# Norm, skip and gating of the recurrent heads: from a stage of their own into the loop over the heads

## What is computed

```python
xc = silu(conv(xm) + conv_b)
h_f = mlstm_chunkwise(q, k, v, g[0], g[1])
h_b = flip(mlstm_chunkwise(flip(q), flip(k), flip(v), flip(g[2]), flip(g[3])))
hs = h_f + h_b                                  # per head, 1024 x 192
mu, var = mean(hs, -1), mean((hs - mu) ** 2, -1)
hs = (hs - mu) * rsqrt(var + LN_EPS)
hs = hs.transpose(...).reshape(B, S, 768) * norm_g
y = (hs + skip * xc) * silu(z)
return concatenate([y, memory_attention(q_mem, mem_k, mem_v)], -1)
```

## Time and profile before

| | us |
|---|---|
| median of three runs (lowest, highest) | 3457.37 (3456.45, 3463.05) |
| the profiled execution, its time | 3455.56 |
| the profiled execution, its span | 3453.8 |
| PE busy in it | 3174.3 (92%) |
| DVE busy | 1901.2 (55%) |
| ACT busy | 1361.8 (39%) |
| POOL busy | 393.6 (11%) |
| granted TensorE clock, mean over the span | 0.959 |

### The profile page before, as it was taken

The page is one execution under the profiler, slowest core; times in us unless marked ns, Lnnn a source line. Parts: engine busy times, 40 slices in busy tenths (PEclk is TensorE's granted clock), DMA queues, the critical chain, the costliest instruction groups (busy, mean ns, idle before and its releaser), DMA issues. The chain is left out here.

```text
span 3453.8 us, 50897 instructions
## 1 busy us (share of the span) xinstructions
PE 3174.3 (92%) x19659; PEld 2529.7 (73%) x19659; DVE 1901.2 (55%) x3571; ACT 1361.8 (39%) x2508; POOL 393.6 (11%) x313
## 2 busy tenths in 40 slices
PE   7999988999989988948799999699989989998999
PEld 6895566888867766747588888488855678895557
DVE  4536746757747725574656647634356543435564
ACT  2006841656652134334156546601344430134451
POOL 0100020333330000002023323200000000000000
PEclk9999998999999999979899999899999999999999
DMA  6518223868866300012368858610000220100012
GB/s 216 186 43 237 67 110 122 353 266 334 341 264 183 111 21 1 1 37 110 132 236 330 330 209 310 239 32 26 25 17 1 100 92 31 38 25 17 1 57 103
DMA packets 192934, 462.48 MB, mean 134 GB/s; under 512 B 44147, under 2 KB 119239, under 8 KB 184137
## 3 DMA queue, kind: packets, MB, share of 16 engines
q1 hardware_dynamic: 174281, 392.35, 31.6%
q0 software_dynamic: 18432, 67.12, 5.1%
HBM read 383.38 MB, written 73.33 MB: 132 GB/s over the span
## 5 line engine op out<-in xcount | busy, mean ns | idle before, releaser
L1790 PE MATMUL psum<-high_in,e_rowsT_high 128*128 128x256 f32 (+1 forms) x1080 | 329.8, 323 | 5.4 <-DVE e_rowsT_low L172 5.4
L1791 PE MATMUL psum<-high_in,e_rowsT_low 128*128 128x256 f32 (+1 forms) x1080 | 326.1, 320 | 0.0
L172 POOL TENSOR_TENSOR low_down<-w_down,high_out 128x1024 fp32r<-128x1024 f32 x64 | 206.7, 3248 | 298.3 <-ACT high_out L1868 298.3
L1790 PEld LDWEIGHTS psum<-high_in,e_rowsT_high 128*128 128x128 f32 x1080 | 206.4, 191 | 22.4 <-issue 6.2
L1791 PEld LDWEIGHTS psum<-high_in,e_rowsT_low 128*128 128x128 f32 x1080 | 206.6, 191 | 16.1
L3607 DVE CUSTOM_DVE_ANT_0 mla_probs<-psum,mla_mask 128x512 f32<-128x512 f32 (+2 forms) x192 | 96.9, 554 | 108.7 <-PE psum L3472 108.1
L172 DVE TENSOR_TENSOR low_gate<-w_gate,high_in 128x1024 fp32r<-128x1024 f32 x128 | 148.0, 1218 | 7.5 <-ACT high_in L1868 6.6
L172 DVE TENSOR_TENSOR low_up<-w_up,high_in 128x1024 fp32r<-128x1024 f32 x128 | 147.9, 1216 | 0.0
L1795 PE MATMUL psum<-low_up,e_rowsT_high 128*128 128x256 f32 x720 | 130.4, 283 | 0.0
L1868 ACT ACTIVATE high_out<-w_down 128x1024 fp32r<-128x1024 f32 x128 | 124.7, 1049 | 7.3 <-DMA w_down<-in_exp_w_down 7.3
L1868 ACT ACTIVATE high_in<-w_gate 128x1024 fp32r<-128x1024 f32 x128 | 124.8, 1058 | 6.2 <-issue 6.2
(11 more groups left out here) (592 smaller groups left out, 7592.0 us busy)
## 6 DMA issues: line engine op xcount, KB each, us to landing
w_gate<-in_exp_w_gate SPq DMA_DIRECT2D x32, 2048.0 KB, 8.4
w_up<-in_exp_w_up SPq DMA_DIRECT2D x32, 2048.0 KB, 13.5
w_down<-in_exp_w_down SPq DMA_DIRECT2D x32, 2048.0 KB, 20.3
ada<-in_ada_w SPq DMA_DIRECT2D x24, 1024.0 KB, 7.6
expert_rows<-e_out POOLq DMA_DIRECT2D x47, 512.0 KB, 7.0
expert_rows<-zero_row SPq DMA_DIRECT2D x33, 512.0 KB, 6.9
token_rows<-x SPq DMA_DIRECT2D x32, 512.0 KB, 2.6
x<-token_rows SPq DMA_DIRECT2D x24, 512.0 KB, 6.9
```

Source lines behind the costliest of these rows:

```text
L172: return eng.tensor_tensor(low, whole, high, ALU.subtract)
L1790: pe.matmul(dst, rows_high[:, k, :], w_high[:, k, cols], start=(k == 0), stop=False)
L1791: pe.matmul(dst, rows_low[:, k, :], w_high[:, k, cols], start=False, stop=False)
```

## The change

The norm's stage is gone; its work is put into the stage of the heads, and the preparation of the next head is put into another order.

- **Preparation.** The spreads go with the qk items of u = 0, 2, 4, 6, the raw items to u = 9 and 10, the keys to u = 8 and 11 to 13. DVE's masks come at u = 1, 3, 5, 7, ACT's exponentials two at a time at u = 4 to 11, `weigh` at u = 12 and 14. Head 0 is prepared in the same order.
- **DVE, every head.** From u = 8 on, the statistics of the unit before and the aggregate of the unit before that. At u = 4 of heads 1 to 3 it inverts the root of the head before, and at u = 6, 8, 9, 10 it normalises two pieces of that head each. After the loop come the last head's norm, and adding and gating for feature tiles 4 and 5.
- **ACT.** A root at u = 2 of heads 1 to 3. In the last head Silu of z at u = 3 to 8, the turned halves of tiles 0 to 3 times the gain into an SBUF tile (`hn_scaled`), and skip times xc for tiles 4 and 5.
- **PE.** In the last head the transposes of tiles 0 to 3, four at a time at eight units; those of tiles 4 and 5 after the loop.
- **GpSimd, new.** For tiles 0 to 3: xc times skip, plus `hn_scaled`, times the gate, each on 128x1024; then the gate of tile 4.
- **SP.** z is loaded in two parts (2 MB when the last keys product of the last head is done, 1 MB after that).

Cut to its core (the removed `head_norm` stands above):

```diff
@@ HeadItems
-        self.steps = [[("qk", u)] for u in range(8)] + [[("keys", m), ("spread", m)] for m in range(4)] + [[("raw", 0)], [("raw", 1)], [], []]
+        self.steps = [[qk[0], spread[0]], [qk[1]], [qk[2], spread[1]], [qk[3]], [qk[4], spread[2]], [qk[5]], [qk[6], spread[3]], [qk[7]],
+                      [keys[0]], [raw[0]], [raw[1]], [keys[1]], [keys[2]], [keys[3]], [], []]
+        self.order = [item for step in self.steps for item in step]
+        self.mask_at = {1: 0, 3: 1, 5: 2, 7: 3}
+        self.weigh_at = {12: 0, 14: 1}
+        self.exponents_at = {4 + n: (2 * n, 2 * n + 1) for n in range(DIRS * TILES // 2)}
@@ heads
+    EARLY_TILES = 4
+    TURN_AT = {4: 0, 5: 1, 7: 2, 8: 3, 10: 4, 11: 5, 12: 6, 13: 7}
+    NORM_AT = {6: (0, 1), 8: (2, 3), 9: (4, 5), 10: (6, 7)}
+    SILU_AT = {3 + f: f for f in range(ML_TILES)}
+    SKIP_AT = {9: 4, 10: 5}
+    late_units = [(4, 0), (5, 0), (4, 1), (5, 1)]
@@ sync
+            sp.wait_ge(s["keys_ready"], 4 * ML_HEADS)
+            sp.dma_start(zT[:, 0:EARLY_TILES, :], core.gate_rows[:, 0:EARLY_TILES, :]).then_inc(s["z_loaded"], 16)
+            sp.wait_ge(s["z_loaded"], 16)
+            sp.wait_ge(s["intra_ready"], U * LAST)
+            sp.dma_start(zT[:, EARLY_TILES:, :], core.gate_rows[:, EARLY_TILES:, :]).then_inc(s["z_loaded"], 16)
@@ tensor
+            def turn(dst, f, half):
+                pe.wait_ge(s["normed"], TILES * last_head_of(f) + 4 * half + 4)
+                for k in range(4):
+                    mm = pe.transpose(dst[:, k * P:(k + 1) * P], features(4 * half + k, f), c["ident"])
+                mm.then_inc(s["turned"], 1)
...
+                    elif u in TURN_AT:
+                        k = TURN_AT[u]
+                        pe.wait_ge(s["keys_copied"], 4 * ML_HEADS)
+                        if k >= 2:
+                            pe.wait_ge(s["scaled"], k - 1)
+                        turn(bank[4 + k % 2], *divmod(k, 2))
@@ scalar
+            def root(h):
+                act.wait_ge(s["variances_ready"], TILES * (h + 1))
+                act.activation(rstd[:, h, :], mv[:, h, :, 1], ACT.Sqrt, bias=c["eps_ln"]).then_inc(s["deviations_ready"], 1)
...
+                    if f >= 2:
+                        act.wait_ge(s["summed"], f - 1)
+                    act.activation(scaled[:, f % 2, half * BANK:(half + 1) * BANK], bank[4 + k % 2], ACT.Copy, scale=gain[:, f:f + 1]).then_inc(s["scaled"], 1)
@@ vector
+                    g = U * h + u
+                    statistics(g - 1)
+                    variance(g - 2)
+                    if h and u == 4:
+                        invert(h - 1)
+                    if h and u in NORM_AT:
+                        normalise(h - 1, NORM_AT[u])
+                    if h < LAST:
+                        prepare(h + 1, u)
...
+            invert(LAST)
+            normalise(LAST, range(TILES))
+            dve.wait_ge(s["skipped"], 2)
+            for n, (f, half) in enumerate(late_units):
+                q = slice(half * BANK, (half + 1) * BANK)
+                dve.wait_ge(s["turned"], 2 * EARLY_TILES + n + 1)
+                dve.scalar_tensor_tensor(out=xcT[:, f, q], in0=bank[4 + n], scalar=gain[:, f:f + 1], in1=xcT[:, f, q], op0=ALU.mult, op1=ALU.add).then_inc(s["added"], 1)
             dve.wait_ge(s["silu_done"], ML_TILES)
...
+            dve.wait_ge(s["added"], 4)
+            dve.tensor_tensor(xcT[:, 5, :], xcT[:, 5, :], zT[:, 5, :], ALU.mult).then_inc(s["gated"], 1)
@@ gpsimd
+            for f in range(EARLY_TILES):
+                x = xcT[:, f, :]
+                pool.tensor_tensor(x, x, skip[:, f:f + 1].to_broadcast([P, SEQ]), ALU.mult).then_inc(s["pool_steps"], 1)
+                pool.wait_ge(s["pool_steps"], f + 1)
+                pool.wait_ge(s["scaled"], 2 * f + 2)
+                pool.tensor_tensor(x, x, scaled[:, f % 2, :], ALU.add).then_inc(s["summed"], 1)
+                pool.wait_ge(s["summed"], f + 1)
+                pool.wait_ge(s["silu_done"], f + 1)
+                pool.tensor_tensor(x, x, zT[:, f, :], ALU.mult).then_inc(s["gated"], 1)
+            pool.wait_ge(s["silu_done"], EARLY_TILES + 1)
+            pool.wait_ge(s["added"], 3)
+            pool.tensor_tensor(xcT[:, 4, :], xcT[:, 4, :], zT[:, 4, :], ALU.mult).then_inc(s["gated"], 1)
```

More of the change, by code:

```diff
@@ L2060, in ml_layer @@
     heads(nc, core, xcT, wq, vals, table, hs)
-    head_norm(nc, core, hs, xcT)
     memT = m.at("ml_memT", W + 40 * KB, [P, 2, SEQ])
@@ L2325, in __init__ @@
     def __init__(self):
[L2326 to L2329, removed]
         self.per_head = {"qk": 8, "keys": 4, "spread": 4, "raw": 2}
-        self.steps = [[("qk", u)] for u in range(8)] + [[("keys", m), ("spread", m)] for m in range(4)] + [[("raw", 0)], [("raw", 1)], [], []]
+        qk, keys, spread, raw = [[(kind, i) for i in range(n)] for kind, n in self.per_head.items()]
+        self.steps = [[qk[0], spread[0]], [qk[1]], [qk[2], spread[1]], [qk[3]], [qk[4], spread[2]], [qk[5]], [qk[6], spread[3]], [qk[7]],
[4 more added lines that the diff above has]
+        self.exponents_at = {4 + n: (2 * n, 2 * n + 1) for n in range(DIRS * TILES // 2)}
     def count(self, kind, H, i):
@@ L2367, in heads @@
     den = m.at("r_den", W + 62 * KB, [P, U])
+    stats = m.at("hn_stats", W + 30 * KB, [P, ML_HEADS, TILES, 6])
+    mv = m.at("hn_mv", W + 30 * KB + 768, [P, ML_HEADS, TILES, 2])
+    rstd = m.at("hn_rstd", W + 31 * KB, [P, ML_HEADS, TILES])
+    gain = m.at("hn_gain", W + 31 * KB + 128, [P, ML_TILES])
+    skip = m.at("hn_skip", W + 31 * KB + 192, [P, ML_TILES])
+    spare = m.at("hn_spare", W + 31 * KB + 256, [P, 1])
+    zT = m.at("hn_z", W, [P, ML_TILES, SEQ])
+    scaled = m.at("hn_scaled", W + 40 * KB, [P, 2, SEQ])
+    LAST = ML_HEADS - 1
+    EARLY_TILES = 4
[4 more added lines that the diff above has]
+    late_units = [(4, 0), (5, 0), (4, 1), (5, 1)]
     bank, c, E = core.bank, core.c, table.E
@@ L2469, in copy_item, with exponents @@
                     act.activation(raw[:, 4 * i:4 * i + 4, :].rearrange("p c q -> p (c q)"), src, ACT.Copy).then_inc(s["raw_copied"], 1)
-            def exponents(H, d):
-                for chunk in range(TILES):
+            def exponents(H, u):
+                for n in items.exponents_at[u]:
+                    d, chunk = divmod(n, TILES)
                     if chunk % 4 == 0:
@@ L2499, in _ @@
                                        scale=E[:, IEXP * S + j:IEXP * S + j + 1]).then_inc(s["carried_ready"], 1)
[L2500 to L2504, removed]
+                    if u == DIRS and h:
+                        root(h - 1)
+                    if u >= 0:
+                        if h < LAST:
+                            prepare(h + 1, u)
+                        else:
+                            finish(u)
+            root(LAST)
         @block.vector
```

159 lines of the change are left out of this document (77 added, 82 removed).

## The result

| | before | after |
|---|---|---|
| median of five runs (lowest, highest) | 3459.68 (3456.45, 3463.05) | 3423.41 (3422.18, 3425.01) |
| the profiled execution, its span | 3453.8 | 3420.5 |
| PE busy | 3174.3 | 3172.5 (93%) |
| DVE busy | 1901.2 | 1906.2 (56%) |
| ACT busy | 1361.8 | 1370.3 (40%) |

The ratio is 0.9896, with a 95% interval from 0.9882 to 0.9909: 36 us faster. The forecast of 3417.3 us was 6 us too low: the time lies in the range from 3398 to 3432, but 1.4 us above the forecast's own range of 3408 to 3422, and next to the 3424 of the first rival.

A forecast was written before the change was run, and what follows sets the result against it. PE bounds heads with a successor, DVE the last head; PE also waits 16.8 us for `weigh`. Gains 23.9 + 32.8, less 16.6 for the port, give 40.1 us: 3417.3 us, own range 3408 to 3422, wider range 3398 to 3432.

The forecast's parts named there:

- first rival: Last head: POOL also holds normalisations and the output below u = 8; 7 us more, 3424; chance 0.18.
- Preparation and boundaries: Stage start to head 3: preparation 28.7, three heads 153.9, boundaries 1.5 us; head 3 starts at 184.1, gaining 23.9.
- Last head without POOL: Last head's 16 units, DVE the bound: 28.3 us, 5.9 added, 4.1 left over from before; together 38.3 us.
- The rest, 8.6 with the barrier: Behind the last head's loop: norm, four additions and a gate, 7.8 us, and the barrier, 0.8.
- The port: Last head and end: POOL operations hold DVE operations with two SBUF tensors; 15 us, plus 1.6 at the end.
- the sign that the prediction set itself: Last head: normalisations and output below u = 8 also showing 2 us and more would mean the first rival holds.
- At the end, gate against gate: After the last head: DVE's gate of tile 5 is held by POOL's gate of tile 4, 1.6 us.
- POOL's median: Last head: POOL's operations were to show a median above 2.36 us.
- the forecast's 247.6 us: The stage: 287.7 us before, less the forecast gain of 40.1 us.
- slower rival: Last head: POOL's chain sets the end from 7.2 us per operation; at 8 us the time is 3467; chance 0.03.
- the boundary wait: Rival, between heads: the order doesn't remove PE's wait for `weigh`; 19 us come back, 3436; chance 0.05.

The follow-up runs named there:

- order_alone: Kernel before with only the new preparation order, the norm keeping its own stage: 3433.75 us, ratio 0.9944.
- pool_tiny: Changed kernel with each of POOL's 13 operations cut to 2 of 1024 columns, leaving work out: 3381.87 us, ratio 0.9785, not usable as a time.
- pool_halves: Changed kernel with each POOL operation done as two of 512 columns, nothing left out: 3415.66 us, ratio 0.9893.
- dve_adds: Changed kernel without POOL: ScalarE skips all six tiles, DVE adds the turned halves from their banks and gates: 3414.52 us, ratio 0.9886.
- skip_on_act: Changed kernel with the skips of tiles 0 to 3 moved from POOL to ScalarE, units 0 to 3 of the last head: 3417.88 us, ratio 0.9894.
- after_again: The changed kernel itself, unaltered, timed once more beside its variants on one chip: 3421.29 us, ratio 0.9900.
- fold: Changed kernel without POOL, the skip folded into the turn by diagonal matmuls on TensorE, DVE finishing each half in one operation: 3415.18 us, ratio 0.9890.
- skip_early: Changed kernel with the skips of tiles 0 to 3 on ScalarE, all in units 0 and 1 of the last head: 3413.41 us, ratio 0.9881.
- fold_early: As fold, with the four diagonal matmuls of the late halves issued ahead of all turns: 3412.04 us, ratio 0.9873.
- norm_alone: Changed kernel with the old preparation order, the norm, skip and gate staying inside the heads' loop: 3445.76 us, ratio 0.9964.

## Why the prediction came out as it did

**Preparation and boundaries** were right. Head 3 was to start at 184.1 us; it does at 184.06 to 184.13 us in order_alone, pool_tiny, pool_halves, dve_adds and skip_on_act. That it fits to 0.1 us is luck, though: two small errors cancel. In order_alone PE is busy for 182.6 us of the 184.1 where my sum has 181.8 (heads take 51.7 us of PE's time for my 51.3), and idle for 1.5 where it has 2.35 (boundaries take 0.3 for my 0.5). In the changed kernel itself it is 188.25, for two reasons outside the sum: 3.3 us of slow clock and 0.9 us of a hold in head 2.

The slow clock first. PE's timeline at the start of the stage, in the changed kernel and then in pool_halves:

```profile
1269.29 2.45 PE L2436 MATMUL psum<-ml_xcT,ml_wqkv 128*96 128x512 f32 x4 [2.94 <-PEq L84]
1271.67 2.07 PE L2447 MATMUL psum<-neg_uT,consts 64*128 64x128 f32 x8
1273.68 5.50 PE L2436 MATMUL psum<-ml_xcT,ml_wqkv 128*96 128x512 f32 x8
```

```profile
1266.17 1.93 PE L2436 MATMUL psum<-ml_xcT,ml_wqkv 128*96 128x512 f32 x4 [2.94 <-PEq L84]
1268.03 1.15 PE L2447 MATMUL psum<-neg_uT,consts 64*128 64x128 f32 x8
1269.11 3.67 PE L2436 MATMUL psum<-ml_xcT,ml_wqkv 128*96 128x512 f32 x8
```

The same instructions behind the same idle time of 2.94 us take 9.8 and 6.55 us; the granted clock is 0.50 (1.2 GHz) for about 6 us in the first and 1.00 in the second. Of the ten traces with the new order four show the drop whole (after, after_again, fold, skip_early), fold_early in half, and five not at all. So the new order alone doesn't bring it, and norm_alone, with the old order, has half of it too (clock 0.94, PE busy 29.54 us for 27.85 before). In the changed kernel it came in both traces, which two traces can't tell from chance. Every trace that reaches the stage later than 1268.6 us has it, and of the others only fold_early (1266.21); whether that means anything no run tests. What decides is open.

**Last head without POOL**: 38.3 was forecast and 39.78 measured in pool_tiny. The missing part is ScalarE: DVE waits 2.4 us for carried copies there, a wait that I put at nothing beside 20 us of busy time in a head. The rest, 8.6 with the barrier, took 9.51: the four additions came 0.81 us apart and not 0.7. That is half of the difference; the rest is spread over the other parts.

**The port**: 15 forecast, 15.6 measured in the last head. That POOL holds DVE was right; which operations it holds was wrong, and the sum was right by luck, with two errors of about one size. I had priced only DVE operations with two SBUF tensors; they lost 9.1 us. The other 6.5 us fell on those with one tensor, the first rival's kinds. By the sign that the prediction set itself, maxima of 2 us and more in the normalisations and in the output below u = 8, it is the first rival that holds. It was right on what is held and wrong on the price: it took the loss for each POOL operation to rise towards 2.0 us, and it was 1.4 (15.6 / 11). In these rows a POOL operation holds DVE at most once, from the start of the first operation of the kinds above, and what DVE does freely between two holds (0.5 us from 1476.30 to 1476.79 above) stays free. At the end, gate against gate, 1.6 was forecast and 1.4 measured (2.61 for 1.22 us).

**The hold in head 2** was left out. POOL's first skip starts as soon as the last keys item is done, at 1454.70, when DVE is in unit 13 of head 2; the output there takes 1.53 us for 0.42, and the head lasts 0.9 us longer. POOL's row, then DVE's:

```profile
1454.70 1.89 POOL L2706 TENSOR_TENSOR ml_xcT<-ml_xcT,hn_skip 128x1024 f32<-128x1024 f32 x1 [220.23 <-PE psum L2441]
```

```profile
1454.82 0.21 DVE L2666 TENSOR_SCALAR r_den<-r_den,exps 128x1 f32<-128x1 f32 x1
1455.07 0.16 DVE L2667 RECIPROCAL r_den<-r_den 128x1 f32<-128x1 f32 x1
1455.27 1.53 DVE L2674 SCALAR_TENSOR_TENSOR ml_hs<-r_num,r_den,ml_hs 128x192 f32<-128x192 f32 x1
```

I had named 12 operations and placed all of them in the last head, where there are 11.

**POOL's median** was to rise above 2.36 us. It didn't: 2.35 for sums and gates and 1.90 for skips. In the last head it was DVE that waited; the most that POOL shows is 2.00 us for a skip of 1.89. One case of the other kind is in pool_halves: there POOL's two halves of the last gate took 3.46 us in place of 2.5, behind DVE's gate.

Together, in the stage against the forecast's 247.6 us: 3.3 clock, 0.9 hold in head 2, 0.8 last head (1.5 more without POOL, less 0.6 since the 15.6 us of holds covered 1.2 of waits), 0.7 rest: 5.7 us, and 1.2 us in the unchanged part ahead of it. The slower rival's condition, 7.2 us for a POOL operation, was never near; nor did the boundary wait stay. That the time came out at the first rival's 3424 is chance: its 7 us more were to come from longer holds, and the largest part of the surplus is the slow clock.

## What to carry to other kernels

An idle GpSimd is not free help for a VectorE that sets the pace: here 11 operations of POOL in the last head cost DVE 15.6 us in holds, while DVE did the adding and gating itself in 10.6, with the skips on ScalarE. Before handing work over, list VectorE's operations with one or two SBUF tensors in that stretch and charge each POOL operation about half its length or more (here 1.4 of 1.9 to 2.4 us). A loop that PE bounds hides preparation and normalisation for the head before, as long as no step of them is in front of PE's next head; the last round, which has no successor, must be summed by itself. And judge a small edit by the stretch it touches: the code around it moved by as much as the edit.

## What the runs showed that was not expected

- A VectorE operation on one column (`r_den`, 159 ns) is held for up to 1.8 us by a POOL operation; a `tensor_scalar` on 192 columns too, one on one column (214 ns) never.
- Cutting a POOL operation in half doesn't halve the loss: 14.4 us with 11 operations in the last head, 11.2 with 22.
- POOL multiplies a 128x1024 tile by one broadcast column in 1.89 to 2.00 us, and by another tile in 2.34 to 2.36.
- The granted clock fell for 6 us, for 3 us or not at all, behind the same 2.94 us of idle PE, in variants that differ only later in the program.
- A kernel with part of a layer left out can change the work of later layers: 8 expert matmuls of 360 in each of several groups vanished, and with them 17 us that have nothing to do with the edit.
